# Output norm of a hybrid decoder layer: three of its batches moved between the HGRN2 products, square roots read from the bank

## The reference

```
x += gate2 * (per-head RMSNorm(concat(group outputs)) @ w_out)
y_a = ssd_mixer(...)        # Mamba-2 SSD,  channels   0..255
y_b = rglru_mixer(...)      # RG-LRU,       channels 256..511
y_c = hgrn2_mixer(...)      # HGRN2,        channels 512..767
y_d = attention             # MLA; prompt causal, sample over 8 cached pages, channels 768..1023

def rms_norm(x, g):
    y = xf * lax.rsqrt(jnp.mean(xf * xf, axis=-1, keepdims=True) + EPS)
    return y * g
```

## Time and profile before

| what | value |
|---|---|
| median of 3 runs | 1911.35 us (1904.53 to 1911.89) |
| the profiled execution | 1913.51 us, its span 1911.8 us |
| PE, share of the span with matmuls | 93% |
| DVE, ACT, POOL | 50%, 32%, 12% |
| mean granted clock of PE | 0.944 of full speed |
| the weave in layer 0, `turn(5)` to the first row of the `w_out` product | 607.16 to 695.13 us |
| the same in layer 1 | 1529.52 to 1613.57 us |

### The profile page before, as it was taken

How to read it: one execution, slowest core, us unless ns; L and a number is a source line. 1 busy time by engine, 2 the same in 40 slices (tenths; PEclk the granted TensorE clock), 3 DMA queues, 4 the chain that set the end, 5 groups by cost and what they waited for, 6 DMA issues and landing times.

```text
span 1911.8 us, 28829 instructions
## 1 busy us (share of the span) xinstructions
PE 1771.8 (93%) x11864; PEld 1524.4 (80%) x11864; DVE 957.6 (50%) x1729; ACT 610.9 (32%) x972; POOL 237.4 (12%) x434
## 2 busy tenths in 40 slices
PE   4999999999989788999989999999998887899998
PEld 3999996667667556999979999967766664699998
DVE  3544432465775644354445444236767745444443
ACT  2433321033231324343334333111433233333331
POOL 8000003510044000000000000072003210000000
PEclk8999999999887889999999999999998788999999
DMA  9566647862011253554453544493201123435542
GB/s 316 192 198 202 207 144 227 272 213 84 1 53 42 101 186 116 166 182 131 162 172 130 178 135 159 149 255 106 93 25 35 38 67 132 132 133 176 169 145 67
DMA packets 206275, 272.06 MB, mean 142 GB/s; under 512 B 11778, under 2 KB 182238, under 8 KB 206144
## 3 DMA queue, kind: packets, MB, share of 16 engines
q1 hardware_dynamic: 188240, 236.90, 37.9%
q0 software_dynamic: 17904, 33.33, 6.1%
HBM read 264.68 MB, written 5.50 MB: 141 GB/s over the span
## 4 chain that ended last, share of the span: by engine, by line
PE 80%; DVE 14%; ACT 3%; DMA 1%; issue 1%; SPq 0%; DVEq 0%; ACTq 0%
PE bank L782 16%; PE bank L784 16%; PE bank L783 16%; PE bank L913 10%; PE bank L1048 4%; PE bank L1309 4%; PE bank L719 2%; DVE sq L2269 2%; PE bank L1221 1%; PE bank L709 1%; DMA ring<-in_w_ada_dram 1%; DVE big L1995 1%; PE bank L1021 1%; PE bank L1191 1%; DVE zs L1628 1%
## 5 line engine op out<-in xcount | busy, mean ns | idle before, releaser
L784 PE MATMUL bank<-hT_r,ring_r 128*128 128x320 f32 x1408 | 440.5, 313 | 0.0
L784 PEld LDWEIGHTS bank<-hT_r,ring_r 128*128 128x128 f32 x1408 | 267.5, 190 | 0.0
L1636 DVE TENSOR_TENSOR ring_r<-ring,lat_pages_r 128x2048 fp32r<-128x2048 f32 (+1 forms) x68 | 151.4, 2229 | 162.4 <-ACT lat_pages_r L1335 162.4
L782 PE MATMUL bank<-hT_r,lat_pages_r 128*128 128x320 f32 x704 | 218.9, 311 | 13.5 <-DVE gates_r L1668 13.5
L783 PE MATMUL bank<-gates_r,lat_pages_r 128*128 128x320 f32 x704 | 219.3, 312 | 0.0
L784 PE MATMUL bank<-big_r,ring_r 128*128 128x320 f32 x704 | 218.0, 310 | 0.0
L913 PE MATMUL bank<-hT,ring 128*128 128x320 f32 x736 | 209.6, 443 | 4.7 <-DVE hT L1662 4.7
L913 PEld LDWEIGHTS bank<-hT,ring 128*128 128x128 f32 x736 | 140.9, 194 | 65.2 <-issue 11.6
L1335 ACT ACTIVATE lat_pages_r<-ring 128x2048 fp32r<-128x2048 f32 (+1 forms) x68 | 126.4, 1862 | 142.8 <-DMA ring<-in_w_ffn_in_dram 69.4
L782 PEld LDWEIGHTS bank<-hT_r,lat_pages_r 128*128 128x128 f32 x704 | 134.0, 190 | 19.0 <-issue 18.5
L783 PEld LDWEIGHTS bank<-gates_r,lat_pages_r 128*128 128x128 f32 x704 | 133.9, 190 | 0.0
(11 more groups left out here) (536 smaller groups left out, 3252.8 us busy)
## 6 DMA issues: line engine op xcount, KB each, us to landing
ring<-in_w_ffn_in_dram SPq DMA_DIRECT2D x88, 1024.0 KB, 6.1
ring<-in_w_ada_dram SPq DMA_DIRECT2D x60, 1024.0 KB, 6.0
ring<-in_w_ffn_out_dram SPq DMA_DIRECT2D x32, 1024.0 KB, 5.2
ring<-in_w_in_dram SPq DMA_DIRECT2D x22, 1024.0 KB, 7.3
sqk<-in_w_ada_dram POOLq DMA_DIRECT2D x24, 512.0 KB, 7.6
ring<-in_w_ffn_out_dram SPq DMA_DIRECT2D x16, 768.0 KB, 4.4
lat_pages<-in_cache_mla_latent_dram POOLq DMA_DIRECT2D x128, 64.0 KB, 2.2
ring<-in_w_out_dram SPq DMA_DIRECT2D x8, 1024.0 KB, 9.2
```

The lines of the kernel that those rows point to most:

```text
L782: mm(out, w_h, x_h, start=start, stop=False)
L784: return mm(out, w_l, x_h, start=False, stop=stop)
L1636: go(v.tensor_tensor(slot_r(n, nk, 256), slot(n, nk, 256), w_hi_r[g % HI][:, 0:nk].bitcast(F32), ALU.subtract), w_low)
```

## The change

The order of `BATCH` becomes SSD, LRU, prompt attention, HGRN2, sample attention. DVE tells the first three `mixed` as soon as the LRU is done, long before. Each batch gets its own room in `sq` (`norm_tmp`), and goes by halves, one chunk at a time, through one bank (bank 7): PE sums one chunk (`out_norm(n, half)`), ACT takes the root straight from the bank, with 1/64 and eps in the same instruction (`on_sqrt`), and only when it is done PE may write the bank again. DVE then inverts the pair and scales (`scale`). `invert` and both `keep_busy` are gone.

```diff
-BATCH = [(0, 0, T), (2, 0, T), (4, 0, T), (6, 0, TP), (6, TP, T)]
+BATCH = [(0, 0, T), (2, 0, T), (6, 0, TP), (4, 0, T), (6, TP, T)]
+BATCH_AT = [0, 640, 0, 1280, 640]
...
+        def norm_tmp(n):
+            _, c0, c1 = BATCH[n]
+            return carve(sq, BATCH_AT[n], 2, T)[:, :, c0:c1]
...
+                    def out_norm(n, half):
+                        if half == 0:
+                            pe.wait_ge(on_sq, at(on_sq, n + 1))
+                        if n or half:
+                            pe.wait_ge(on_root, at(on_root, 2 * n + half))
+                        _, c0, c1 = BATCH[n]
+                        mm(bank[7][:, c0:c1], c("ones64"), norm_tmp(n)[:, half], start=True, stop=True).then_inc(on_pe, 1)
...
                     score(4)
-                    keep_busy(14)
+                    out_norm(0, 0)
                     turn(5)
+                    out_norm(0, 1)
                     pe.wait_ge(hg_dve, at(hg_dve, 7))
                     block_sums(2).then_inc(hg_pe, 1)
+                    out_norm(1, 0)
                     from_states(0, 0, 0).then_inc(hg_pe, 1)
+                    out_norm(1, 1)
                     from_states(1, 1, 0)
+                    out_norm(2, 0)
                     from_states(2, 1, 256).then_inc(hg_pe, 1)
+                    out_norm(2, 1)
                     score(5)
-                    keep_busy(20)
                     soft_turn(2)
                     soft_spread(2)
-                    out_norm(0)
+                    out_norm(3, 0)
                     tail(1)
+                    out_norm(3, 1)
                     value(2)
                     value_taken(2)
                     turn(6)
-                    out_norm(1)
-                    tail(1)
+                    tail(2)
                     score(6)
                     tail(2)
-                    out_norm(2)
                     turn(7)
...
                     score(7)
-                    out_norm(3)
                     tail(4)
...
                     tail(3)
-                    out_norm(4)
-                    tail(2)
+                    out_norm(4, 0)
+                    tail(1)
+                    out_norm(4, 1)
+                    tail(1)
...
+                    def on_square(n):
+                        ac.wait_ge(mixed, at(mixed, n + 1))
+                        k0, c0, c1 = BATCH[n]
+                        if n == 2:
+                            ac.wait_ge(on_scaled, at(on_scaled, 1))
+                        o.go(f(norm_tmp(n), hT[:, k0:k0 + 2, c0:c1], ACT.Square), on_sq)
+
+                    def on_sqrt(n):
+                        _, c0, c1 = BATCH[n]
+                        for half in range(2):
+                            ac.wait_ge(on_pe, at(on_pe, 2 * n + half + 1))
+                            o.go(f(norm_tmp(n)[:, half], bank[7][:, c0:c1], ACT.Sqrt, bias=eps, scale=1.0 / 64), on_root)
...
                     att_copy(4)
+                    on_square(0)
+                    on_square(1)
                     att_squares(4)
                     att_root(4)
+                    on_sqrt(0)
                     att_copy(5)
+                    on_sqrt(1)
+                    on_square(2)
+                    on_sqrt(2)
                     att_squares(5)
...
+                    def scale(n):
+                        k0, c0, c1 = BATCH[n]
+                        x = norm_tmp(n)
+                        ve.wait_ge(on_root, at(on_root, 2 * n + 2))
+                        do(v.reciprocal(x, x))
+                        for k in range(k0, k0 + 2):
+                            y = hT[:, k, c0:c1]
+                            go(v.scalar_tensor_tensor(y, y, col("out_norm", k), x[:, k - k0], MUL, MUL), on_scaled if k > k0 else None)
+
+                    scale(0)
+                    scale(1)
                     ve.wait_ge(hg_pe, at(hg_pe, 5))
                     add_from_states(0, 0, 0)
...
                     do(v.tensor_tensor(hT[:, 4:6], oacc, gh, MUL))
-                    for n in range(4):
-                        o.tell(mixed)
+                    o.tell(mixed)
+                    scale(2)
                     att_inv(5)
```

More of the change, by code:

```diff
@@ L105 @@
        "cq_copied": 1, "att_t": 8, "att_tc": 8, "att_k": 64, "att_sq": 64, "att_q": 8, "ones_ready": 1, "att_in": 8, "att_rk": 8, "att_mix": 8,
-       "soft_pe": 12, "soft_dve": 20, "soft_act": 4, "group_used": 4, "on_pe": 5, "on_sq": 5, "on_inv": 5, "on_root": 5,
+       "soft_pe": 12, "soft_dve": 20, "soft_act": 4, "group_used": 4, "on_pe": 10, "on_sq": 5, "on_root": 10,
        "on_scaled": 5, "wo_done": 8, "wo_used": 8, "mla_act_in": 2, "mla_root": 2, "prob_act": 8, "wkr_ready": 1,
@@ L431, in trunk @@
         on_sq = sem("on_sq")
-        on_inv = sem("on_inv")
         on_root = sem("on_root")
@@ L1288, in _ @@
                     value_taken(3)
+                    pe.wait_ge(on_root, at(on_root, 8))
                     for h in range(4):
@@ L1562, in _ @@
                     att_copy(4)
+                    on_square(0)
+                    on_square(1)
                     att_squares(4)
                     att_root(4)
+                    on_sqrt(0)
                     att_copy(5)
+                    on_sqrt(1)
+                    on_square(2)
+                    on_sqrt(2)
                     att_squares(5)
                     att_root(5)
[L1570 to L1580, removed]
-                    for n in range(4):
-                        on_square(n)
+                    on_square(3)
+                    on_sqrt(3)
                     soft_exp(2)
-                    on_sqrt(0)
                     att_copy(6)
-                    on_sqrt(1)
                     att_squares(6)
@@ L1596, in _ @@
                     soft_exp(3)
-                    on_sqrt(3)
                     on_square(4)
+                    on_sqrt(4)
                     tail_copy(2)
-                    on_sqrt(4)
                     tail_copy(3)
@@ L2162, in _ @@
                     go(v.tensor_copy(lh_last[:, :, 1:NQ], lh[:, :, TP:T].rearrange("p j (b t) -> p j b t", b=NB)[:, :, :, TS - 1]), lru_dve)
-                    go(v.tensor_tensor(hT[:, 2:4], lh, gelu, MUL))
+                    do(v.tensor_tensor(hT[:, 2:4], lh, gelu, MUL))
+                    for n in range(3):
+                        o.tell(mixed)
                     go(v.tensor_tensor(wf, wf, kh, MUL), hg_dve)
@@ L2261, in _ @@
                     soft_max(2)
[L2263 to L2277, removed]
                     soft_row(2)
                     soft_less(2)
-                    invert(0)
+                    scale(3)
                     soft_values(2)
-                    scale(0)
-                    invert(1)
                     att_inv(6)
                     att_scores(6)
-                    scale(1)
-                    invert(2)
                     tail_add(0)
                     att_inv(7)
-                    scale(2)
                     att_scores(7)
@@ L2296, in _ @@
                     tail_add(1)
-                    invert(3)
                     soft_values(3)
-                    scale(3)
                     ve.wait_ge(mla_pe, at(mla_pe, 12))
                     do(v.tensor_copy(hT[:, 6:8, TP:T], bank[7][:, 0:128].rearrange("p (j n) -> p j n", j=2)), mixed)
-                    invert(4)
                     scale(4)
```

1 line of the change is left out of this document (removed).

## The result

The changed kernel takes 1918.2 us (median of 13 runs) against 1911.35 before. The ratio is 1.0044, interval 1.0028 to 1.0059, that is 8.4 us longer, 5 to 11; the two medians differ by 6.9, inside that interval. The time lies inside the predicted range, and the change is smaller than the 0.5% that I counted as no change, but it goes the other way: -3 was forecast.

What follows compares the result with a forecast made beforehand. PE's list sets the end; in the weave ending each mixer no engine is full and time goes into handing over. Stage sums of -3.6 and +0.4 us give -3.2: from 1911.35 to 1908, range 1895 to 1919.

Steps and rivals of the forecast that it cites:

- the unhidden norm: DVE's third batch late for `score(5)`'s end: each layer gives back up to 4.1 us, time 1916; chance 0.04.
- Stage 1: From `turn(5)` to `soft_turn(2)`: five `out_norm` products join PE's list, +5.4 us in each layer.
- the second rival: Clock falls before `from_states`: half clock for all of this stretch, +11.0 us per layer, time about 1921; chance 0.10.
- the sign of being wrong that I had named: The stretch from `turn(5)` to `soft_turn(2)` outside 31 to 37 us, which would be the clock.
- both gaps: PE idle 2.7 us behind `score(4)` and 5 us ahead of `soft_turn(2)`; half clock behind both would decide for 1921.
- The loss of the cover: Before `turn(5)`: 3.23 us of unread products go, one product of 0.67 stands in, PE idles some 2.7 us.
- Stage 2: From `soft_turn(2)` to `turn(6)`: the exponential waits for the fourth batch's roots; 12.5 us taken, +3.7 and +2.9 by layer.
- Stage 3: From `turn(6)` to `value(3)`: the gain, -10.0 us in layer 0 and -8.0 in layer 1.
- the stops: Waits of 3.73 and 2.76 us inside `score(6)` and `score(7)`, forecast to go, below 0.5 us there.
- the 1.0 of DVE's multiplications: Between `turn(6)` and `value(3)`: 1.0 us of multiplications in DVE's chain, counted as gone.
- Stage 4: From `value(3)` to the first row of the `w_out` product: -2.7 us in layer 0, +0.1 in layer 1.
- The third rival: DVE's work loses its cover beside `from_states` or `score(5)`: up to 4.1 us back per layer, time 1916; chance 0.04.

Runs made afterwards that it cites:

- two later executions: The changed kernel with no edit, profiled twice more: 1915.22 and 1920.15 us, where its first profiled execution took 1911.96.
- before_no14: The kernel before without its 14 unread products behind `score(4)`, the 20 ahead of `soft_turn(2)` kept: 1921.93 us, ratio 1.0065 to the kernel before.
- states_fill: The changed kernel plus an unread 64-column product behind every 8 products of `from_states`, 20 in all: 1944.50 us, ratio 1.0152 to the kernel before.

## Why the prediction was wrong

The direction was wrong. That 1918 lies inside the range is luck: its upper end was there for the unhidden norm, which did not happen.

**Stage 1, the step that failed first.** "I take the clock to fall at about the same moment as now" holds in the first execution, in both layers, and even there the stage is +6.3, not +5.4. The five products take 4.9 us by their starts, not 4.4: at half clock one of 320 columns is 1.36 between the small products (613.75 to 615.11), where I took 1.17, half of a pair. The 320 rows take 15.4 in place of 13.4 (I had +1.0 for that), and `score(5)` is 0.5 shorter. In the two later executions the gap ahead of `turn(5)` lowers the clock before `from_states` begins, in both layers. In layer 1 it comes back in time and the stage is +6.1; in layer 0 it is +8.1 and, where the clock stays down to the end of the rows, +10.9. That is the second rival, at the +11.0 that it was priced at, and the sign of being wrong that I had named (39.15, outside 31 to 37), in one layer of six. I gave it 0.10 and wanted both gaps and both layers for it; each can come alone.

The loss of the cover was named but priced at nothing. In before_no14, which changes in nothing else, it costs some 12 us of 1910 by the median, of which the trace shows 6.6 in layer 1's weave and none in layer 0's; in the changed kernel its return gives some 3. The Trainium skill (TensorE: Matmul & The Clock Gate, Why this matters for your kernels) warns of idle gaps of PE between bursts of matmuls, but only of longer ones than this. The traces differ from it: the 2.65 us were followed by a lower clock in nine of the 14 layers with this gap, and not in five.

**Stage 2.** The chain was the one described: two roots, a load, the exponential, and `turn(6)` behind it. I took 12.5 us between 10.5 and 13.4; it is 13.3 to 14.5, at or beyond the slow end: the gap ahead of `soft_turn(2)` brings the clock down in every execution of the changed kernel. `value(2)` starts at 8.2 to 9.0, where 8.3 was that end. The choice inside the bounds was most of the error, which is 1.4 and 1.3.

**Stage 3** came as forecast: the stops are gone, the clock stays up in all but one layer, -10.2 in the mean of layer 0 (forecast -10.0), -7.6 in layer 1 (-8.0; my own terms add up to -8.5). That the sum for layer 0 fits is in part luck. The products behind the two stops gained all of the 2.3 of which I took half, and `out_norm(3)` left the stage too, 1.1 (675.27 to 676.34 before), which I had not counted; the 1.0 of DVE's multiplications that I did count shows nowhere in PE's timeline, and the stops gave 6.1, not 6.5.

**Stage 4.** Layer 0 -2.2 (forecast -2.7), layer 1 +1.2 to +1.3 (+0.1). I counted half of the 1.65 that `value(3)` would gain in layer 1 at full clock; it takes 3.65 as before. Moving the one load takes 0.8 to 1.0 off, less than the 1.28 counted. The Trainium skill (ScalarE: Activation LUTs, What ACT_TABLE_LOAD costs) adds a drain to each load. The trace does not show it: in the rows of `soft_exp(2)` above, the exponential begins 0.01 behind the load's end.

**The third rival fell.** DVE, in the changed kernel, ends its third batch and then waits for ACT's squares of `score(5)` twice, the second time ahead of the last sum, so it is not late:

```profile
631.87 0.88 DVE L2271 SCALAR_TENSOR_TENSOR hT<-hT,par,sq 128x256 f32<-128x256 f32 x2
632.66 1.27 DVE L2006 TENSOR_REDUCE big<-sqk 128x8 f32<-128x512 f32 x2
634.30 0.69 DVE L2006 TENSOR_REDUCE big<-sqk 128x8 f32<-128x512 f32 x1 [0.36 <-ACTq L471]
635.66 0.69 DVE L2006 TENSOR_REDUCE big<-sqk 128x8 f32<-128x512 f32 x1 [0.67 <-ACTq L471]
```

So the errors have one sign. In the mean of the three executions, layer 0 and 1 lie above the forecast by 3.0 and 0.8 us in stage 1, by 1.4 and 1.3 in stage 2 and by 0.5 and 1.2 in stage 4, with 0.2 left over from stage 3: 8.3 in all, and -3.2 becomes +5.1. What is missing from there to the 8.4 of the runs stays open.

## What to carry to other kernels

Work that nobody reads can stand on the path all the same, for what runs behind it: before it is dropped, price the rows behind the gap at the lower clock, and count a gap that "may" lower it as one that does in some executions. Work moved into an idle time should not be put in front of the one instruction that others wait for: here two roots ahead of an exponential cost some 9 us in the two layers, half of the 18 that stage 3 gained. Where a product goes into a list of sparse ones (small products that use part of the array, as in `from_states`) at half clock, look for a wait at full clock to put it in.

## What the hardware showed that I had not expected

The same idle time of 2.65 us ahead of the same instruction is followed by 1.09 us in one execution and 1.97 in another; what decides is not shown by these runs. Twenty dense products strewn among the sparse ones did not hold the clock up: in states_fill, layer 0, it is 0.50 in every stretch read from 620 to 645 us. And a 128 x 128 product of 64 columns set between 64 x 64 products of 8 columns takes 0.43 us of PE at full clock, some 0.2 more than its share in a run of its like; what in the change between the two kinds takes that time is not shown.
